# Reordering the first norm and the products of u: square one step ahead, scale and transposes one step later, products two steps later, by a written-out plan

## The reference, cut to what matters

```python
def _rmsnorm(x, g):
    xf = x.astype(jnp.float32)
    y = xf * lax.rsqrt(jnp.mean(xf * xf, axis=-1, keepdims=True) + EPS)
    return (y * g.astype(jnp.float32)).astype(x.dtype)
...
    proj = xn @ w_in.astype(xn.dtype)                                  # (N, T, N_IN)
    pa, pb, pg = jnp.split(proj, [2 * C_A, 2 * C_A + 2 * C_B], axis=-1)
...
    z = jax.nn.gelu(pb, approximate=False)
    u, v = jnp.split(z, 2, axis=-1)
    v_n = _layernorm(v, ln_b_g, ln_b_b)                                # (N, T, C_B)
    y_b = (u * _chunk_spatial_mix(v_n, w_s, b_s)) @ w_b_out.astype(xn.dtype)
```

## Time and profile before

| | |
|---|---|
| time, median of 3 runs | 1130.21 us (1129.7 to 1131.74) |
| profiled execution, its own time | 1128.82 us |
| span of its slowest core (core 0) | 1127.2 us |
| spans of the eight cores | 1121.0 to 1127.2 us |
| PE busy over the span | 1072.0 us (95%) |
| DVE, ACT, POOL busy over the span | 621.6, 438.4, 191.5 us |
| granted PE clock, mean of core 0 | 0.994 |

### The profile page before, as it was taken

The page is one execution under the profiler, slowest core; times in us unless marked ns, Lnnn a source line. Parts: engine busy times, 40 slices in busy tenths (PEclk is TensorE's granted clock), DMA queues, the critical chain, the costliest instruction groups (busy, mean ns, idle before and its releaser), DMA issues.

```text
span 1127.2 us, 18952 instructions; the slowest of 8 cores (1121.0 to 1127.2 us)
## 1 busy us (share of the span) xinstructions
PE 1072.0 (95%) x6502; PEld 613.1 (54%) x6591; DVE 621.6 (55%) x1220; ACT 438.4 (39%) x798; POOL 191.5 (17%) x401
## 2 busy tenths in 40 slices
PE   3889998999999999999999989999999999999997
PEld 2646445666776555555555545555555555444443
DVE  3343898667678633333446666666666666333332
ACT  2443453122484711111135555555555555111111
POOL 2143110007382100010001211111111111000000
PEclk9989999999999999999999999999999999999999
DMA  9658404000033122242258722333333322443331
GB/s 219 197 86 122 82 1 78 17 15 15 16 53 57 20 39 38 38 76 38 39 163 273 225 46 47 58 56 57 57 57 57 58 47 38 126 149 107 111 106 70
DMA packets 36285, 88.87 MB, mean 79 GB/s; under 512 B 4128, under 2 KB 6304, under 8 KB 36192
## 3 DMA queue, kind: packets, MB, share of 16 engines
q0 software_dynamic: 21552, 38.75, 21.6%
q1 hardware_dynamic: 14640, 48.92, 13.4%
HBM read 108.05 MB, written 20.04 MB: 114 GB/s over the span
## 4 chain that ended last, share of the span: by engine, by line
PE 85%; DVE 5%; issue 4%; DMA 2%; ACT 2%; POOL 1%; DVEq 0%; SPq 0%; POOLq 0%; ACTq 0%
PE ps L303 83%; PE ps L306 2%; DVE arena L327 2%; DMA arena<-x_p 2%; DVE arena L619 1%; ACT arena L314 1%; DVE arena L317 1%; ACT arena L311 1%; DVE arena L322 1%; POOL arena L317 1%; DMA arena<-col_f 1%; POOL arena L180 0%; DVE arena L622 0%; DVEq L194 0%; DVE arena L324 0%
## 5 line engine op out<-in xcount | busy, mean ns | idle before, releaser
L303 PE MATMUL ps<-arena 128*128 128x512 bf16 (+6 forms) x5958 | 1043.8, 335 | 21.7 <-DVE arena L317 10.0
L303 PEld LDWEIGHTS ps<-arena 128*128 128x128 bf16 (+1 forms) x6047 | 580.4, 102 | 468.5 <-issue 31.3
L314 ACT ACTIVATE arena<-ps 128x224 f32<-128x224 f32 (+7 forms) x356 | 178.8, 515 | 319.6 <-PE ps L303 238.3
L327 DVE SCALAR_TENSOR_TENSOR arena<-arena 128x64 f32<-128x64 bf16 (+5 forms) x540 | 253.8, 505 | 37.6 <-POOL arena L317 15.4
L314 ACT ACTIVATE arena<-arena 128x512 f32<-128x512 f32 (+4 forms) x185 | 121.3, 673 | 192.4 <-DVE arena L327 170.5
L327 DVE SCALAR_TENSOR_TENSOR arena<-arena,ps 128x512 f32<-128x512 f32 (+4 forms) x120 | 70.1, 589 | 162.0 <-PE ps L303 154.1
L317 DVE TENSOR_TENSOR arena<-arena,ps 128x512 bf16<-128x512 f32 (+2 forms) x143 | 86.6, 615 | 84.4 <-ACT arena L314 84.4
L311 ACT ACTIVATE arena<-arena 128x1024 bf16<-128x1024 f32 (+2 forms) x52 | 53.9, 1037 | 159.2 <-DVE arena L317 138.2
L317 DVE TENSOR_TENSOR arena<-ps,arena 128x1024 bf16<-128x1024 bf16 (+4 forms) x72 | 65.1, 908 | 83.8 <-PE ps L303 75.0
L317 POOL TENSOR_TENSOR arena<-arena 128x1 f32<-128x1 f32 (+2 forms) x73 | 43.8, 600 | 374.4 <-DVE arena L324 272.5
L180 POOL DMA_DIRECT2D arena<-w_all x138 | 74.9, 556 | 190.7 <-PE ps L303 175.9
(11 more groups left out here) (19 smaller groups left out, 32.6 us busy)
## 6 DMA issues: line engine op xcount, KB each, us to landing
arena<-w_all POOLq DMA_DIRECT2D x138, 256.0 KB, 5.5
arena<-x_p SPq DMA_DIRECT2D x32, 512.0 KB, 7.5
h1s<-arena SPq DMA_DIRECT2D x16, 512.0 KB, 4.2
arena<-h1s SPq DMA_DIRECT2D x16, 512.0 KB, 4.1
o_yp<-arena SPq DMA_DIRECT2D x15, 512.0 KB, 2.9
o_ch<-st_a SPq DMA_DIRECT2D x1, 1664.0 KB, 17.8
arena<-dw_t POOLq DMA_DIRECT2D x4, 384.0 KB, 4.6
arena<-st_a POOLq DMA_DIRECT2D x1, 960.0 KB, 12.3
```

The costliest lines, as they stand in the source:

```text
L303: S.op("pe", lambda q: q.matmul(out, lhsT=lhsT, rhs=rhs, start=start, stop=stop), [out], [lhsT, rhs], inc=stop)
L314: S.op("act", lambda q: q.activation(out=out, in_=in_, func=func, scale=scale, bias=bias), [out], ins)
L327: S.op("dve", lambda q: q.scalar_tensor_tensor(out=out, in0=in0, scalar=scalar, in1=in1, op0=op0, op1=op1), [out], [in0, in1] + ([scalar] ...
```

## The change

`sq` is split: its first part is only the square on ACT, and the mean and the power go to `sq_rstd`. `first`, `um`, `xstep`, `work` and `at` are gone. A single `nstep(c)` records, in this order, the square of c, the scale of c-1, the mean and power of c, the transposes of c-1 and the evacuation of c-1. Behind each of the steps 2 to 17 come the products that `PLAN` lists for it. These use only chunks up to c-2, except in step 17, whose second and third groups need chunk 16. The first column block of a pair of chunks is computed in two products of 128 columns for j = 0 and 1 in some steps; the later ones have 256, 512, 288 or 320 columns. The setup pieces hang on steps: `setup_dma` behind step 8, two loads of `vW` behind each of steps 9 to 12, `setup_mask` behind step 12, `setup_v` behind step 14 and `setup_bias` behind step 15.

```diff
             s = slot()
             sstat[c] = s
             act(junk[c % 2][:cs], xbuf[c % NXB][:cs], AF.Square, accum=s[:cs, 0:1])
+
+        def sq_rstd(c):
+            cs = rows(c)
+            s = sstat[c]
             tsc("dve", s[:cs, 1:2], s[:cs, 0:1], 1.0 / D, EPS, ALU.mult, ALU.add)
             rstd_of(s[:cs, 1:2], s[:cs, 2:3], cs)
...
-        nstep = [8]
-        nready = [0]
-
-        def xstep():
...
+        def nstep(c):
+            if c < 17:
+                sq(c)
+            if 1 <= c <= 17:
+                xscale(c - 1)
+            if c < 17:
+                sq_rstd(c)
+            if 1 <= c <= 17:
+                xtr(c - 1)
+                norm_evac(c - 1, 34)
...
-        def first(c):
...
-        first(0)
-        first(1)
-        norm_evac(1, 34)
-        um(0, (0,))
...
-        at = {0: 8, 2: 9, 5: 10, 8: 11, 10: 12, 11: 13, 13: 14, 15: 15, 17: 16, 19: 17, 21: 18}
-        for n, (c0, w, j) in enumerate(work):
-            while nready[0] < -(-(c0 + w) // 128) and nready[0] < 17:
-                xstep()
-            u_mm(c0, w, j)
...
+        A1, A2 = 128, 256
+        PLAN = {
+            2: [(0, A1, (0, 1))],
+            3: [(128, A1, (0, 1)), (0, A2, (2,))],
+            4: [(0, A2, (3,)), (256, A1, (0, 1))],
+            5: [(384, A1, (0, 1)), (256, A2, (2,)), (0, A2, (4,))],
+            6: [(256, A2, (3, 4)), (0, A2, (5,))],
+            7: [(512, A2, (0, 1, 2))],
+            8: [(0, A2, (6, 7)), (256, A2, (5, 6))],
+            9: [(256, A2, (7,)), (512, 512, (3, 4))],
+            10: [(512, 512, (5, 6))],
+            11: [(512, 512, (7,)), (768, A2, (0, 1))],
+            12: [(768, A2, (2,)), (1024, A2, (0, 1, 2))],
+            13: [(1280, A2, (0, 1, 2)), (1024, 512, (3,))],
+            14: [(1024, 512, (4, 5))],
+            15: [(1024, 512, (6, 7))],
+            16: [(1536, A2, (0, 1, 2, 3))],
+            17: [(1536, 288, (4, 5, 6, 7)), (1792, 320, (0, 1, 2, 3)), (1824, 288, (4, 5, 6, 7))],
+        }
+        nstep(0)
+        nstep(1)
+        for c in range(2, 18):
+            nstep(c)
+            for c0, w, js in PLAN[c]:
+                for j in js:
+                    u_mm(c0, w, j)
+            if c == 8:
                 setup_dma()
-            if 3 <= n < 11:
-                vW.append(load_unit(V0 + n - 3, OFF_C + 16384 + 2048 * (n - 3)))
-            if n == 14:
+            if 9 <= c < 13:
+                for i in range(2):
+                    vW.append(load_unit(V0 + len(vW), OFF_C + 16384 + 2048 * len(vW)))
+            if c == 12:
                 setup_mask()
-            if n == 20:
+            if c == 14:
                 setup_v()
-            if n == 24:
+            if c == 15:
                 setup_bias()
```

More of the change, by code:

```diff
@@ L524, in u_mm @@
             act(u[:, j, c0:c0 + w], psb(b)[:, 0:w], AF.Gelu)
-        def first(c):
[L528 to L536, removed]
-        first(0)
-        first(1)
-        norm_evac(1, 34)
-        um(0, (0,))
[L542 to L579, removed]
-        at = {0: 8, 2: 9, 5: 10, 8: 11, 10: 12, 11: 13, 13: 14, 15: 15, 17: 16, 19: 17, 21: 18}
-        for n, (c0, w, j) in enumerate(work):
-            while nready[0] < -(-(c0 + w) // 128) and nready[0] < 17:
-                xstep()
-            u_mm(c0, w, j)
-            if n in at and nstep[0] <= at[n]:
-                xstep()
-            if n == 1:
+        A1, A2 = 128, 256
```

## The result

The changed kernel takes 1123.3 us (median) against 1130.2 before. The ratio is 0.9936 with an interval of 0.992 to 0.9951: 7.2 us, 0.64% less. The forecast was 1121.4, its range 1118.0 to 1126.5.

What follows compares the result with a forecast made beforehand. TensorE was taken to idle 21.5 us in the u stage, waiting for scaled chunks and evacuations. Walking the queues, with 8.4 us of uncovered setup and 1.7 of low clock, ended it 8.8 us earlier: 1121.4, range 1118.0 to 1126.5.

Steps and rivals of the forecast that it cites:

- The place and the direction: TensorE's slack lies in the u stage, 21.5 us idle; the new order ends that stage 8.8 us earlier.
- waits for evacuations: In the u stage, products wait 6.4 us for evacuated transposes; the new order removes these waits.
- chain of 4.0 us: From a step's last products through Gelu, Square, mean, evacuation and scale to transposes; light steps stall, cover complete from 3.6.
- The setup ahead of the scale: Setup on DVE after steps 12, 14 and 15 delays a scale PE waits for: 1.25, 4.3 and 2.8 us.
- The low clock: The idle array before step 15 loses the clock once, costing 1.7 us, with bounds 0 and 1.9.
- the walk: Step-by-step times of u-stage products and transposes worked out along the queues, ending at T17 = 96.95 us.
- the rival with two falls: The pause before step 16 also loses the clock, 1.7 us more: 1123.1; chance 0.22, shared with a late clock rise.
- The start: The first steps of u are bound by DMA; step 3's products start at the low clock and end at 22.2.
- late rise: Low clock at the start lasting through step 4 costs 1.3 us, through step 5 3.7; chance 0.22, shared with two falls.
- The rival that the early level stays low: Steps 3 to 7 of u stay at 1.2 GHz, 4.5 us slower overall: 1134.7; chance 0.07.
- the gain is swallowed later: A fixed-time transfer holds a stage after u, so nothing is left of the gain: 1130.2; chance 0.09.

Runs made afterwards that it cites:

- norm in line: The changed kernel with the norm of a chunk no longer spread over steps, plan of products and setup places kept: 1191.7 us.
- the square's lead: The changed kernel with the square of c+1 recorded in step c, ahead of the products of c: 1118.8 us.
- late setup: The changed kernel with setup_mask, setup_v and setup_bias moved behind products of step 17: 1111.9 us.
- filler runs: The changed kernel with work nobody reads behind setup_v and setup_bias: 1116.9 us with matmuls, 1118.8 us with transposes.
- filler matmuls: The changed kernel plus matmuls of 512 columns that nobody reads, 16 behind setup_v and 8 behind setup_bias: 1116.9 us.
- filler transposes: The changed kernel plus transposes of 128x128 that nobody reads, 64 behind setup_v and 32 behind setup_bias: 1118.8 us.
- bias late: The changed kernel with only setup_bias moved, behind the second group of step 17: 1119.0 us.

## Why the prediction was right, and where its terms were off

**The place and the direction.** Right. The slack was in this stage, the 6.4 us of waits for evacuations went whole, the later stages carried the shift unchanged. The norm in line shows the converse: with the chain of 4.0 us uncovered the stage takes 67 us more.

**The chain of 4.0 us.** Right in size (4.2 where it stands bare in the norm in line, with PE idle 4.05) and in effect: light steps stall by 0.2 to 1.0 us, heavy ones not, and cutting it by the square's lead removed the later of these stalls, 1.6 us on average over the cores.

**The setup ahead of the scale.** Right in mechanism, slightly high in size: pauses of 4.08, 2.51 and 0.95 us against 4.3, 2.8 and 1.25, 7.5 against 8.4. The late setup less the filler runs comes to the same 7.5.

**The low clock.** This is the term that was mis-sized. The forecast had one fall at 1.7 us. On core 0 the clock fell twice. Behind the first pause, step 15's products took 5.8 us (70.01 to 0.27 ahead of the Gelu at 76.10) instead of 3.46, and the transposes 0.37 more: 2.7. Behind the second, 6.0 instead of 3.48 and again 0.37: 2.9. From the end of step 14 to the end of u core 0 took 34.1 us (64.4 to 98.5), the walk had 30.0.

The other cores differ. With filler matmuls DVE's queue is the same and the clock stays high; there the step behind the first pause takes 7.12 us from transposes to transposes on every core, the one behind the second 4.03. What each takes longer in after is the price of the clock, in us:

| core | 0 | 1 | 2 | 3 | 4 | 5 | 6 | 7 |
|---|---|---|---|---|---|---|---|---|
| behind the first pause | 2.7 | 2.8 | 2.7 | 2.9 | 1.7 | 1.7 | 1.7 | 2.9 |
| behind the second | 2.9 | 2.9 | 2.9 | 1.3 | 0.0 | 0.0 | 0.0 | 1.3 |

The mean is 3.8 in all, and the end of u of the filler run says 3.9. So one fall at 1.7 is just what cores 4, 5 and 6 paid, while cores 0, 1 and 2 paid 5.6, among them the two slowest (1 and 2), and the time is that of the slowest. The granted clock shows how the prices differ. On core 0 it was low from 68.0, 1.2 us before the pause ended, to about 74.8. On core 4 the pause ended at 70.78 with the clock still high; it was low only from about 71.2 to 74.6:

```profile
68.00:70.00 2.00, 0.00 (x0) 0.00 (x0) 1.51 (x7) 0.00 (x0) 0.00 (x0) 1.00 0.00 0
70.00:72.00 2.00, 1.22 (x10) 0.83 (x11) 1.11 (x3) 0.00 (x0) 0.55 (x1) 0.79 0.00 0
72.00:74.00 2.00, 2.00 (x6) 0.76 (x5) 0.81 (x1) 0.00 (x0) 0.00 (x0) 0.50 0.00 0
74.00:76.00 2.00, 2.00 (x10) 0.81 (x8) 0.00 (x0) 0.60 (x1) 0.00 (x0) 0.86 0.00 0
```

I sized the fall from the products at 69.19 in the earlier trace rows. There the clock was low by 66 us, and while PE idles in front of its products, the low clock costs nothing; on core 0 of after only 1.2 us of the low stretch fell in the pause. What decides how long after the start of a pause the clock falls, and so which core pays what, isn't shown.

Of the named cases the rival with two falls comes nearest (1123.1, measured 1123.3). Two falls did come on five of the cores, but they cost 1.3 to 2.9 us each and not 1.7, so that its number is so near is in part luck.

**The start.** The walk had the fourth chunk's transposes (X3) at 22.2; core 0 had them at 20.3. The profiled execution of before had a late start on that core (transposes at 9.36; 8.46 in after). Core 1, on the other hand, had its step-3 products at the low speed:

```profile
18.99 3.62 PE L303 MATMUL ps<-arena 128*128 128x128 bf16 x24
```

against 1.93 on core 0, where these products ran at high speed from 17.38 on. The granted clock of the profile doesn't show this early level; it reads 1.00 on core 1 in the middle of the slow products, so that here the durations have to be read:

```profile
20.00:21.00 1.00, 1.00 (x11) 0.94 (x9) 1.00 (x2) 0.28 (x2) 0.00 (x0) 1.00 1.08 217
```

With a landing of x that was 1.2 us later on core 1 (third chunk's transposes at 18.18, against 16.94), it made the start of that core 2.9 us longer (fifth chunk's at 26.37, against 23.47), and core 1 the slowest: 101.5 against 98.5 at the end of u. The two errors of the walk, 2.6 us too late at step 14 and 4.1 too short behind it, partly cancelled; the sum was 1.5 us short on core 0. That the forecast came within 1.9 us of the time was in part this luck. The prices of a late rise were also low by the walk's own rules: the low level through step 4 would cost 2.0 us in it, not 1.3, and through step 5 4.15 (33.4 less 29.25), not 3.7; the range would have held either.

**The rival that the early level stays low**, 1134.7, didn't come: the latest rise in after, by the durations, was near 23 us, on core 1. **That the gain is swallowed later** is refuted: the v stage takes 80.3 us on every core of every run, whatever the start, but for the norm in line (80.6), and what follows takes 939.0 us in before and after.

**The rule on transposes** of the Trainium skill ("TensorE: Matmul & The Clock Gate", Part 4), which stood behind the rival with two falls, says that transpose mode doesn't count as a busy PE in the way matmuls do. The run with filler transposes contradicts it: they hold the clock up as well as matmuls, on all eight cores. So the rule pointed at the second fall for a wrong reason. That fall goes when its pause goes (bias late) or is filled; why it came on five cores and not on three isn't settled.

## What to carry to other kernels

When work is spread over pipeline steps, everything else on the same in-order queue becomes part of the pipeline. Look for one-off work (constants, masks, bias tables) that used to run behind the loop and now stands in front of an instruction that the bottleneck engine waits for; moving three such pieces gave 11 us where the reordering had given 7. Price a pause of the matrix engine with the clock behind it, and to measure that price put idle matmuls into the pause.

## What the runs showed of the hardware that I hadn't expected

A pause of 4.1 us cost a further 2.7 to 2.9 us in the work behind it on five cores, and 1.7 on three, where the clock fell only once the work had begun again and was back sooner. A pause of 2.5 us, coming some 6 us later, cost 2.9 us on three cores, 1.3 on two and nothing on three. Transposes alone, 64 in 3.75 us, kept the granted clock at 1.00. Before the early rise, which came near 23 us at the latest, the granted clock of the profile reads 1.00 while the matmuls take the time of 1.2 GHz. Adding 24 matmuls of 512 columns that nobody reads made the stage 3.9 us shorter. And the stages behind v, the same program in each run, took between 935.5 and 945.5 us on the cores from the end of the v stage on, which is why the slowest of eight tells less of a change in one stage than the end of that stage does.
